# A hybrid-mixer encoder: GpSimd arithmetic taken out of the mixer, whose steps are reordered, and a first weight unit in two pieces

## The reference, cut to what matters

```
proj = h @ w_in[l]
lru_x, lru_g, sq, sk, sv, dq, dk, dv = split(proj)
# recurrent: 4-tap convolution of lru_x, two sigmoid gates, a linear scan, times gelu(lru_g)
# swa: 4 heads, 2 key heads, 128-token window, sink in the softmax
# diff: 4 heads, out = (softmax0 - lam * softmax1) @ v, RMS norm per head
x = x + rms_norm(concat(y_lru, y_swa, y_diff) @ w_out[l], gain)
```

## Time and profile before

| what | us |
|---|---|
| median of 3 runs | 1042.76 (1040.89 to 1043.97) |
| the profiled execution | 1041.41 |
| its span | 1039.6 |
| TensorE busy | 990.3 (95% of the span) |
| VectorE busy | 685.2 |
| ScalarE busy | 517.6 |
| GpSimd busy | 58.3 |

### The profile page before, as it was taken

How to read it: one execution, slowest core, us unless ns; L and a number is a source line. 1 busy time by engine, 2 the same in 40 slices (tenths; PEclk the granted TensorE clock), 3 DMA queues, 4 the chain that set the end, 5 groups by cost and what they waited for, 6 DMA issues and landing times.

```text
span 1039.6 us, 13313 instructions
## 1 busy us (share of the span) xinstructions
PE 990.3 (95%) x5426; PEld 854.1 (82%) x5426; DVE 685.2 (66%) x894; ACT 517.6 (50%) x682; POOL 58.3 (6%) x66
## 2 busy tenths in 40 slices
PE   4999999999799999999999999999997999999997
PEld 3888888788787888888888888887887888888886
DVE  4765756676857676665677666657686778655654
ACT  3654444455455554444565444444571656454542
POOL 0130000000500400000000000000031100000000
PEclk8999999999779999999999999999995999999999
DMA  8588655455224566655447656554641236656651
GB/s 267 163 248 282 199 190 177 168 173 183 81 82 154 150 207 200 201 180 185 162 144 241 211 175 200 185 181 161 203 139 65 81 122 223 202 173 192 195 170 41
DMA packets 131516, 180.84 MB, mean 174 GB/s; under 512 B 4112, under 2 KB 114840, under 8 KB 131456
## 3 DMA queue, kind: packets, MB, share of 16 engines
q1 hardware_dynamic: 129200, 176.24, 51.8%
q0 software_dynamic: 2256, 3.76, 1.7%
HBM read 178.92 MB, written 2.63 MB: 175 GB/s over the span
## 4 chain that ended last, share of the span: by engine, by line
PE 81%; DVE 8%; ACT 5%; issue 3%; DMA 2%; DVEq 0%; POOL 0%; ACTq 0%; POOLq 0%
PE UP L423 31%; PE Y L445 21%; PE UP L425 15%; PE Y L435 2%; DVE wlo L1006 2%; PE Y L473 2%; ACT whi L740 1%; PE Y L467 1%; DVE x L1060 1%; PE Y L468 1%; PE Y L572 1%; DMA raw<-in_w_in 1%; PE UP L453 1%; DMA raw<-in_ffn_w_up 1%; DVE xs L1055 1%
## 5 line engine op out<-in xcount | busy, mean ns | idle before, releaser
L423 PE MATMUL UP<-xT,whi 128*128 128x512 f32 x1520 | 543.6, 401 | 3.5 <-DVE dqk L1215 2.7
L1006 DVE TENSOR_TENSOR wlo<-raw,whi 128x2048 fp32r<-128x2048 f32 x160 | 367.9, 2299 | 146.9 <-ACT whi L740 146.8
L425 PE MATMUL UP<-xT,wlo 128*128 128x256 f32 x1520 | 428.1, 282 | 0.0
L740 ACT ACTIVATE whi<-raw 128x2048 fp32r<-128x2048 f32 x160 | 305.9, 1912 | 104.2 <-DMA raw<-in_ffn_w_gate 76.4
L423 PEld LDWEIGHTS UP<-xT,whi 128*128 128x128 f32 x1520 | 287.5, 189 | 75.1 <-issue 2.8
L425 PEld LDWEIGHTS UP<-xT,wlo 128*128 128x128 f32 x1520 | 289.1, 190 | 1.3
L445 PE MATMUL Y<-whi,yT 128*128 128x512 f32 x736 | 207.6, 392 | 0.0
L445 PEld LDWEIGHTS Y<-whi,yT 128*128 128x128 f32 x736 | 135.1, 188 | 27.9
L445 PE MATMUL Y<-wlo,yT 128*128 128x512 f32 x368 | 114.2, 392 | 0.0
L820 ACT ACTIVATE gate_small<-UP 128x512 f32<-128x512 f32 x40 | 23.8, 595 | 116.8 <-PE UP L425 116.8
L445 PEld LDWEIGHTS Y<-wlo,yT 128*128 128x128 f32 x368 | 69.0, 188 | 15.6
(11 more groups left out here) (188 smaller groups left out, 860.9 us busy)
## 6 DMA issues: line engine op xcount, KB each, us to landing
raw<-in_ffn_w_gate SPq DMA_DIRECT2D x44, 1024.0 KB, 5.4
raw<-in_ffn_w_up SPq DMA_DIRECT2D x44, 1024.0 KB, 5.4
raw<-in_ffn_w_down SPq DMA_DIRECT2D x44, 1024.0 KB, 4.9
raw<-in_w_in SPq DMA_DIRECT2D x20, 1024.0 KB, 5.1
raw<-in_w_out SPq DMA_DIRECT2D x8, 1024.0 KB, 4.8
gains<-in_ffn_norm_pre SPq DMA_DIRECT2D x4, 512.0 KB, 6.0
gains<-in_ffn_norm_post SPq DMA_DIRECT2D x4, 512.0 KB, 5.8
shift_scratch<-shift_rows POOLq DMA_DIRECT2D x1, 1536.0 KB, 13.3
```

Of the source, the lines that this page charges most:

```text
L423: nc.tensor.matmul(dst[:, 0:2 * S], h[:, kt, c:c + P], xT[:, kt, :, :].rearrange("p h s -> p (h s)"), start=kt == 0, stop=False, skip_grou ...
L425: mm = nc.tensor.matmul(dst[:, S:2 * S], o[:, kt, c:c + P], xT[:, kt, 0, :], start=False, stop=kt == KT - 1, skip_group_check=True)
L740: A.activation(whi[:, k % RING, :], raw[:, k % RING, :], ACT.Copy).then_inc(hi_ready, 1)
L1006: V.tensor_tensor(wlo[:, k % RING, :], raw[:, k % RING, :], whi[:, k % RING, :].bitcast(F32), ALU.subtract).then_inc(lo_ready, 1)
```

## The change

The unit of `lru_x` moves ahead of the queries. The convolution and the gelu's product move from GpSimd to VectorE (`conv`, `gelu_cube`); GpSimd keeps its DMAs and the masks of the bias. Both gates, their tanhs, the decays and their root come early, and the scan follows the first job's logits. A tile is accumulated by three matmuls of 256 columns in one half bank, and ScalarE copies it straight to its place; VectorE's add is gone. `swkv` is done by token in both tiles; its keys are copied twice side by side (`kdup`) and turned (`turn_keys`, `keys_copy`). Jobs' steps stand in another order; `softmax_logits` signals its two halves apart; `softmax_weights` does the subtraction in four operations instead of eight, and the norm's epsilon takes up the division. `laminit` and one of its DMAs go, constants stand in its place. A square-root table load comes at the end of the mixer. At the start the first weight unit comes in two DMAs and is split in two pieces, the second unit is loaded ahead of the second half of `x` and split ahead of its norm, the warm-up doubles, and the bias product follows both first units on token tile 0.

```diff
-IN_ORDER = ((DV, 0), (DV, 1), (DQ, 0), (DK, 0), (DQ, 1), (DK, 1), (LRU_X, 0), (SWQ, 0), (SWKV, 0), (LRU_G, 0))
+IN_ORDER = ((DV, 0), (DV, 1), (LRU_X, 0), (DQ, 0), (DK, 0), (DQ, 1), (DK, 1), (SWQ, 0), (SWKV, 0), (LRU_G, 0))
 IN_UNITS = len(IN_ORDER)
-U_DQ0, U_DK0, U_DQ1, U_DK1, U_LRU_X, U_SWQ, U_SWKV, U_LRU_G = range(2, 10)
...
+        KEYS = bank(Y, 0)
...
-            load_cols(0, a["ffn1_w_gate"], 0, 0)
+            for h in range(2):
+                sp.dma_start(cols(0, raw)[:, 4 * h:4 * h + 4, :],
+                             a["ffn1_w_gate"][0, HALF * h:HALF * h + HALF, 0:UC].rearrange("(k p) n -> p k n", p=P)).then_inc(raw_loaded[0] if h else first_loaded, 16)
+            load_cols(1, a["ffn1_w_up"], 0, 0)
             sp.dma_start(x[:, 1, :], a["x"][0, P:2 * P, :]).then_inc(x_loaded[1], 16)
...
-                link(G.tensor_tensor(lru_conv[:, :, :], lx[:, :, 0:S], per_tile(PC_CONV, 4), ALU.mult))
-                    link(G.tensor_tensor(pool_tmp[:, :, :], lx[:, :, tap:tap + S], per_tile(PC_CONV + tap, 4), ALU.mult))
-                    link(G.tensor_tensor(lru_conv[:, :, :], lru_conv[:, :, :], pool_tmp[:, :, :], ALU.add))
-                G.tensor_tensor(lru_conv[:, :, :], lru_conv[:, :, :], per_tile(PC_CB), ALU.add).then_inc(conv_ready, 1)
-                link(G.tensor_tensor(lru_gsq[:, :, :], lru_gsq[:, :, :], lg[:, :, :], ALU.mult))
-                G.tensor_tensor(lru_gsq[:, :, :], lru_gsq[:, :, :], lg[:, :, :], ALU.add).then_inc(g_cubed, 1)
...
+            for l in range(1, L):
+                small_parameters(l)
...
                     for kt in range(KT):
+                        if k == t == kt == 0:
+                            pe.wait_ge(first_hi, 1)
+                            pe.wait_ge(first_lo, 1)
+                        elif k == t == 0 and kt == 4:
+                            unit_ready(k)
...
+                if s == 0:
+                    pe.wait_ge(consts_loaded, 32)
+                    nc.tensor.matmul(UP[0:8, 0:SHIFTS], table[:, :], onehot[:, :], start=True, stop=True).then_inc(vec_done, 1)
+                else:
                     pe.wait_ge(x_half, quarter(s - 1, 1, 0) + 1)
...
+                if s == 0:
+                    pe.wait_ge(vec_copied, 1)
...
+            def turn_keys(l):
+
+                wait_tile_copied(pe, l, U_SWKV, 1)
+                pe.wait_ge(logits_ready, 2 * (l * JOBS + JOB_B) + 2)
+                for t in range(NT):
+                    for h in range(2):
+                        tr = nc.tensor.transpose(KEYS[:, S * h + P * t:S * h + P * t + P], kdup[:, t, P * h:P * h + P], ident[:, :])
+                tr.then_inc(keys_turned, 1)
...
+            def lru_gates(l):
+                pe.wait_ge(conv_ready, l + 1)
+                for g in range(2):
+                    for t in range(2):
+                        mm = nc.tensor.matmul(GATES[g][:, S * t:S * t + S], lruw[:, t, g, :], lru_conv[:, t, :],
+                                              start=True, stop=True)
...
-                    if u > U_DQ0 and not (u - 1 == U_SWKV and t == 1):
-                        wait_tile_read(pe, l, u - 1, t)
-                    elif u > U_DQ0:
-                        wait_values_copied(pe, l, 5)
-                    dst = bank(UP, t)
-                    if u == U_SWKV and t == 1:
-                        for tok in range(NT):
-                            for kt in range(KT):
-                                xh, xl = (xT[:, kt, i, tok * P:(tok + 1) * P] for i in range(2))
-                                h, o = cols(k, whi)[:, kt, P:2 * P], cols(k, wlo)[:, kt, P:2 * P]
-                                nc.tensor.matmul(dst[:, P * tok:P * tok + P], xh, h, start=kt == 0, stop=False)
-                                nc.tensor.matmul(dst[:, P * tok:P * tok + P], xh, o, start=False, stop=False)
-                                mm = nc.tensor.matmul(dst[:, P * tok:P * tok + P], xl, h, start=False, stop=kt == KT - 1)
-                    else:
-                        mm = feature_tile(dst, k, P * t)
+                    if u > U_LRU_X:
+                        wait_tile_copied(pe, l, u - 1, t)
+                    dst, h, o = bank(UP, t, 0, S), cols(k, whi), cols(k, wlo)
+                    for kt in range(KT):
+                        if u == U_SWKV:
+                            tok = slice(t * P, t * P + P)
+                            products = (xT[:, kt, 0, tok], h[:, kt, :]), (xT[:, kt, 0, tok], o[:, kt, :]), (xT[:, kt, 1, tok], h[:, kt, :])
+                        else:
+                            col = slice(t * P, t * P + P)
+                            products = (h[:, kt, col], xT[:, kt, 0, :]), (h[:, kt, col], xT[:, kt, 1, :]), (o[:, kt, col], xT[:, kt, 0, :])
+                        for n, (stat, mov) in enumerate(products):
+                            mm = nc.tensor.matmul(dst, stat, mov, start=kt == n == 0, stop=kt == KT - 1 and n == 2)
...
+                in_tile(U_LRU_X, 0)
+                in_tile(U_LRU_X, 1)
                 in_tile(U_DQ0, 0)
                 in_tile(U_DQ0, 1)
                 in_tile(U_DK0, 0)
+                lru_gates(l)
                 in_tile(U_DK0, 1)
                 in_tile(U_DQ1, 0)
                 scores(l, JOB_A)
                 in_tile(U_DQ1, 1)
                 in_tile(U_DK1, 0)
                 in_tile(U_DK1, 1)
-                in_tile(U_LRU_X, 0)
+                in_tile(U_SWQ, 0)
+                pe.wait_ge(gates_tanh, l + 1)
+                turn_weights(l, JOB_A)
                 scores(l, JOB_B)
-                in_tile(U_LRU_X, 1)
-                turn_weights(l, JOB_A)
-                in_tile(U_SWQ, 0)
+                in_tile(U_SWQ, 1)
                 values(l, JOB_A)
-                in_tile(U_SWQ, 1)
                 in_tile(U_SWKV, 0)
+                in_tile(U_SWKV, 1)
                 turn_output(l, JOB_A)
-                in_tile(U_SWKV, 1)
+                in_tile(U_LRU_G, 0)
+                turn_keys(l)
                 pe.wait_ge(mix_lo, l * OUT_UNITS + 1)
                 turn_weights(l, JOB_B)
                 scores(l, JOB_SWA)
-                in_tile(U_LRU_G, 0)
+                in_tile(U_LRU_G, 1)
                 values(l, JOB_B)
-                lru_gate(l, 0)
-                in_tile(U_LRU_G, 1)
-                lru_gate(l, 1)
-
-                pe.wait_ge(logits_ready, l * JOBS + JOB_SWA + 1)
+
+                pe.wait_ge(logits_ready, 2 * (l * JOBS + JOB_SWA) + 2)
                 out_ready(OUT_A, 1)
                 both_banks(out_unit(OUT_A), mixed(OUT_A), 0, True)
-                wait_tile_read(pe, l, U_LRU_G, 1)
+                both_banks(out_unit(OUT_A), mixed(OUT_A), 1, True).then_inc(unit_used, 1)
                 turn_output(l, JOB_B)
-                both_banks(out_unit(OUT_A), mixed(OUT_A), 1, True).then_inc(unit_used, 1)
+                wait_tile_copied(pe, l, U_LRU_G, 1)
+                turn_weights(l, JOB_SWA)
...
-            keep_clock(6)
-            pe.wait_ge(consts_loaded, 32)
-            nc.tensor.matmul(UP[0:8, 0:SHIFTS], table[:, :], onehot[:, :], start=True, stop=True).then_inc(vec_done, 1)
-            pe.wait_ge(vec_copied, 1)
+            keep_clock(12)
...
+            def split_first(h):
+                act.wait_ge(raw_loaded[0] if h else first_loaded, 16)
+                part = slice(1024 * h, 1024 * h + 1024)
+                A.activation(whi[:, 0, part], raw[:, 0, part], ACT.Copy).then_inc(hi_ready if h else first_hi, 1)
...
-                    if s == 0 and t == 1:
-                        split(1)
+                    if s == t == 0:
+                        split_first(0)
                     for h in range(2):
                         if not (s and t == 0 and h == 1):
                             turned_hi(s, t, h)
-                    if s == 0 and t == 0:
-                        split(0)
+                    if s == t == 0:
+                        split_first(1)
+                        split(1)
 
...
+                    src = bank(UP, t, 0, S)
+                    if u == U_SWKV:
+                        keys = src[:, 0:P].rearrange("p (h d) -> p h d", h=2).unsqueeze(2).to_broadcast([P, 2, 2, HD])
+                        A.activation(kdup[:, t, :].rearrange("p (h c d) -> p h c d", h=2, c=2), keys, ACT.Copy)
+                        ins = A.activation(swv[:, t, :], src[:, P:2 * P], ACT.Copy)
+                    else:
+                        dst = {U_LRU_X: lx[:, t, 3:3 + S], U_LRU_G: lg[:, t, :], U_SWQ: swq[:, t, :],
+                               U_DQ0: dqk[:, t, :], U_DQ1: dqk[:, 2 + t, :],
+                               U_DK0: dqk[:, 4 + t, :], U_DK1: dqk[:, 6 + t, :]}[u]
+                        ins = A.activation(dst, src, ACT.Copy)
+                    ins.then_inc(tile_copied, 1)
+
+                def keys_copy():
+                    act.wait_ge(keys_turned, l + 1)
+                    A.activation(swk[:, :, :], KEYS.rearrange("p (h s) -> p h s", h=2), ACT.Copy).then_inc(keys_copied, 1)
...
```

(100 more changed lines are left out.)

217 lines of the change are left out of this document (85 added, 132 removed).

## The result

The changed kernel takes 1002.4 us (median of 4 runs, 1001.62 to 1003.56), the kernel before in the same measurement 1043.37 us. The ratio is 0.9611, with a 95% interval of 0.96 to 0.9623. The prediction was 1002 us, with a range of 994 to 1016. The profiled execution took 1003.56 us, its span is 1001.8 us.

What follows compares the result with a forecast made beforehand. The prediction took TensorE's stall for `att` and the half clock after it, over 16 us a mixer, as the largest loss. 1042.76 - 38 (two mixers) - 2.7 (start) = 1002.1 us; range 994 to 1016.

Steps and rivals of the forecast that it cites:

- The wait ahead of `turn_output`: Each mixer, TensorE waiting for VectorE's `att` of job A: goes once GpSimd's arithmetic is gone, -6.1 us.
- Part 1 of the prediction: VectorE's chain to `att`: loses 4.7 us of drawing out, and some 2 to 5 us of work ahead of it.
- layout: New orders laid out by hand per engine with the trace's durations, for one mixer: -20 us end to end.
- The half clock: Each mixer, behind the stall: not entered; second `swkv` tile -7.4 us, the next 10.7 us of work -5.3.
- Three matmuls of 256 columns: Fifteen tiles of each mixer: three matmuls take 0.36 us where a pair took 0.352, +1.0 us.
- The adds: Each mixer: TensorE's two waits for VectorE's add of a tile go, -1.4 us.
- The keys' transposes: Each mixer, new work on TensorE: four transposes of the keys, +0.45 us.
- VectorE's and ScalarE's new work: Each mixer: convolution under 3.9 us on VectorE and two more table loads of 1.28 us on ScalarE, all hidden.
- The tail: End of each mixer: job SWA's 1.7 us wait becomes 1.4 and 1.3, both behind VectorE's weight pieces, +1.0 us.
- Per mixer, -19: Whole gain of one mixer, taken as -19 us from a sum of -17.8 and a layout of -20; bounds -15 and -21.6.
- The start: Ahead of token tile 1: it starts at about 26.1 us against 28.82, -2.7 us, bounds -1.3 and -4.2.
- new stall: Rival: `att` of job A late by some 4 us, half clock again, 9 us a mixer given back, 1020 us; chance 0.14.

Runs made afterwards that it cites:

- The filled wait: The kernel before with 26 idle products put ahead of `turn_output` of job A, so TensorE is busy while `att` is late: 1023.81 us, ratio 0.9818.
- the tail's first reordering: The kernel after with VectorE's logits of job SWA moved ahead of weight piece 11 and its weights ahead of piece 12: 1004.23 us.

## Why the prediction was right, point by point

*The wait ahead of `turn_output`, -6.1 us.* Right: none is left, -6.2. The cause as predicted is shown from both sides, by the kernel before without the convolution on GpSimd (6.2 to 1.4) and by GpSimd's work put back (0.16 to 0.75 us for one operation). In the kernel before GpSimd's arithmetic accounts for 4.8 of the 6.2; the last 1.4 falls to the new order. Part 1 of the prediction credits that order with some 2 to 5 us by which VectorE's chain starts earlier. It doesn't: the reduction starts at 269.86 us against 269.04 before, since the logits of job B come later too. What the order gives is that TensorE comes to `turn_output` 3.2 us later, which the prediction has in its layout only. What the new order would give with GpSimd computing through the whole chain no run shows: the work put back overlapped it for 2.8 us only.

*The half clock, -7.4 and -5.3 us.* Right. The filled wait prices the clock alone at 9.4 a mixer. The prediction's 12.7 also holds the change of shape. At full clock the second `swkv` tile goes from 48 x 0.11 = 5.3 us to 24 x 0.12 = 2.9: 2.4 us, and with it the 9.4 make 11.8, against -12.7.

*Three matmuls of 256 columns, +1.0.* The size of a pass is right: the first five tiles, 120 matmuls, take 14.40 us, 0.120 each. This is the row of that stretch in the kernel after:

```profile
224.97:239.37 14.40, 14.40 (x122) 14.40 (x121) 11.01 (x12) 7.33 (x8) 0.00 (x0) 1.00 0.88 291
```

*The adds, -1.4.* Right: no wait for a tile's copy is left in the mixer.

*The keys' transposes, +0.45.* Right: they start at 277.21 and the next matmul at 277.64, 0.43 us.

*VectorE's and ScalarE's new work, nothing.* Right. The convolution takes 3.5 us on VectorE, in the kernel after as in the kernel before with it there, under the 3.9 of the bound. For the tables, the kernel without the root's loads shows no change. In the kernel after the first exponential starts right behind its load (252.79 and 1.28 us long):

```profile
252.79 1.28 ACT L886 ACT_TABLE_LOAD   x1
254.08 0.51 ACT L886 ACTIVATE prob<-logit,sm 128x256 f32<-128x256 f32 x1
```

By the rule of the Trainium skill that the prediction names ("ScalarE: Activation LUTs", What ACT_TABLE_LOAD costs) a drain comes with each load; no run here shows it.

*The tail, +1.0.* Half wrong, in a term of 1 us. It had waits of 1.4 and 1.3 in place of 1.7; they measured 0.5 and 1.4, so +0.2. The step that failed is "both behind VectorE's weight pieces": for the weights it holds, for the logits it doesn't, as the tail's first reordering showed.

*Per mixer, -19.* Measured -18.8 in the profiled execution. From the times, (1042.9 - 1002.35 - 3.5)/2 = 18.5, where 1042.9 is about the median of the kernel before over the measurements. The terms as measured (-6.2, -11.8, +1.0, -1.4, +0.45, +0.2) add up to -17.8. Which term hides the missing 0.7 to 1.0 us stays open.

*The start, -2.7.* The step sizes were right (`xs` at 8.53 for 8.2, the second unit at 18.83 for 18.5). Token tile 1 came at 27.28 us in one execution and at 25.44 in the other, around the predicted 26.1, which assumed the half clock. From the second unit to token tile 1 it has 7.6 us, the executions 8.45 and 7.66. The gain, 3.5 us by the times (3.1 and 4.0 in the two measurements) and 2.5 by where the first mixer begins, lies on both sides of the 2.7 and inside its bounds. That every 1 us reaches the end holds as far as times of four runs can tell.

*The rivals.* No new stall: `att` is ready, though with no slack. Where one was made on purpose, 2.0 us long, a mixer lost 3 us and not 9; a stall of 4 us wasn't tried. In the mixers of the new order the clock was never at half for longer than 3.4 us.

So the two terms that carry the sum, the stall and its half clock, were each within a tenth of what was measured. That the total came out within 0.5 us is luck in part. The listed terms gave -17.8 a mixer, and with them the forecast would have been 1004.5 us; the 19 was taken between that sum and the layout's 20. And small errors cancel: the mixers gave up to 0.5 us each less than the 19, the start by the times 0.8 us more than its 2.7. The lower end of the range is also misadded: 2 x 21.6 + 4.2 less than 1042.76 is 995.4, not 994.

## What to carry to other kernels

When one engine idles for microseconds ahead of a late small chain, look at what the other engines did while the chain ran, not only at its own length: tiny operations of many times their usual length are the sign. Look also at when the waiting engine arrives: here half of the wait went because TensorE came later, with useful work put ahead. Price a stall with the half clock behind it as a range, and fill it with idle products to see the two apart. When a small step moves ahead of a bulk piece, look for the next small step still behind that piece: moving one traded a wait of 1.4 us for one of 1.8, and only moving both removed them.

## What the hardware showed that I had not expected

The fall of the clock behind a short wait is not a fixed price. The same 1.4 us of idling, in the same place of two mixers, was followed by full clock in one and by 17.1 us at half in the other; 2.0 us of idling by full clock in one and 3.4 us at half in the other. And the same program spent 3.4 or 6.8 us at half clock in its start, which moved its token tile 1 by 0.8 us.

GpSimd's arithmetic touched VectorE's chained 128x4 operations unevenly: beside it one took 0.75 us, and its neighbours 0.17. The wide ones show less: the reduction from 128x512 beside GpSimd took 0.69 us, as it does without it. But a weight piece took 3.05 instead of 2.28, and GpSimd's own additions were drawn out as well while VectorE worked on weight pieces. Two equal ones in the kernel before, the first beside a weight piece:

```profile
263.67 3.29 POOL L402 TENSOR_TENSOR xs<-xs,pool_tmp 128x512 f32<-128x512 f32 x1
...
270.09 1.29 POOL L402 TENSOR_TENSOR xs<-xs,pool_tmp 128x512 f32<-128x512 f32 x1
```
